# First token half's products issued ahead of the second half's transposes at the block ends

## The reference, cut to what matters

```python
def layer_norm(x, g, b):
    xf = x.astype(jnp.float32)
    mu = jnp.mean(xf, axis=-1, keepdims=True)
    var = jnp.mean(jnp.square(xf - mu), axis=-1, keepdims=True)
    return ((xf - mu) * lax.rsqrt(var + LN_EPS) * g + b).astype(x.dtype)

for i in range(DEPTH_2):                                      # DEPTH_2 = 2
    x = layer_norm(ALPHA * x + 0.5 * swiglu(x, ...), ...)     # ffn1
    proj = x @ rwkv_w_in[j]                                   # i = 0;  x @ sb_w_in[j] for i = 1
    ...
    x = layer_norm(ALPHA * x + heads @ w_out[i], ...)
    x = layer_norm(ALPHA * x + 0.5 * swiglu(x, ...), ...)     # ffn2
```

## Time and profile before

| | us |
|---|---|
| median of 3 runs | 1456.42 (1456.1 to 1458.33) |
| profiled execution, its own time | 1456.55 |
| its span in the trace | 1454.8 |
| PE busy | 1414.5 (97% of the span) |
| PEld busy | 1290.6 (89%) |
| DVE busy | 952.5 (65%) |
| ACT busy | 683.7 (47%) |
| granted TensorE clock, mean | 0.998 of full |

### The profile page before, as it was taken

How to read it: one execution, slowest core, us unless ns; L and a number is a source line. 1 busy time by engine, 2 the same in 40 slices (tenths; PEclk the granted TensorE clock), 3 DMA queues, 4 the chain that set the end, 5 groups by cost and what they waited for, 6 DMA issues and landing times.

```text
span 1454.8 us, 31311 instructions
## 1 busy us (share of the span) xinstructions
PE 1414.5 (97%) x12733; PEld 1290.6 (89%) x12733; DVE 952.5 (65%) x1290; ACT 683.7 (47%) x880; POOL 156.9 (11%) x182
## 2 busy tenths in 40 slices
PE   6999999999999999999989999999999999999997
PEld 5868799999999998988879999999999898899996
DVE  3657786667655556795786655675656778855656
ACT  5455654455433436743435433454334476534332
POOL 1442033221000004021300000000000011000000
PEclk9999999999999999999999999999999999999999
DMA  8975566666666645321036666566666344576662
GB/s 349 355 291 203 158 210 183 189 196 177 175 188 184 191 143 183 116 89 61 4 113 201 180 187 195 166 202 188 187 189 186 125 139 162 158 218 183 187 190 85
DMA packets 293910, 257.76 MB, mean 177 GB/s; under 512 B 7104, under 2 KB 270272, under 8 KB 290752
## 3 DMA queue, kind: packets, MB, share of 16 engines
q1 hardware_dynamic: 293824, 256.49, 57.5%
HBM read 255.42 MB, written 1.05 MB: 176 GB/s over the span
## 4 chain that ended last, share of the span: by engine, by line
PE 50%; DVE 4%; ACT 1%; issue 0%; DVEq 0%; ACTq 0%
PE ps L145 14%; PE ps L146 14%; PE ps L147 14%; PE ps L2331 3%; PE ps L383 1%; DVE stats L342 1%; DVE arena L340 1%; PE ps L390 1%; PE ps L469 0%; PE ps L474 0%; PE ps L470 0%; PE ps L2314 0%; PE ps L2322 0%; DVE gate_m L2634 0%; PE ps L2817 0%
## 5 line engine op out<-in xcount | busy, mean ns | idle before, releaser
L145 PE MATMUL ps<-actT,a_parts 128*128 128x256 f32 x2096 | 588.3, 281 | 2.9 <-DVE a_parts L130 2.0
L146 PE MATMUL ps<-actT,a_parts 128*128 128x256 f32 x2096 | 585.0, 279 | 0.0
L147 PE MATMUL ps<-actT,a_parts 128*128 128x256 f32 x2096 | 584.9, 279 | 0.0
L145 PEld LDWEIGHTS ps<-actT,a_parts 128*128 128x128 f32 x2096 | 394.0, 188 | 12.1 <-issue 3.8
L146 PEld LDWEIGHTS ps<-actT,a_parts 128*128 128x128 f32 x2096 | 393.8, 188 | 4.2
L147 PEld LDWEIGHTS ps<-actT,a_parts 128*128 128x128 f32 x2096 | 393.9, 188 | 0.0
L1350 DVE TENSOR_TENSOR a_parts<-a_raw,a_parts 128x2048 fp32r<-128x2048 f32 x100 | 238.4, 2384 | 54.5 <-ACT a_parts L1347 54.1
L1364 DVE TENSOR_TENSOR b_parts<-b_raw,b_parts 128x1024 fp32r<-128x1024 f32 x72 | 88.3, 1226 | 160.3 <-ACT b_parts L1361 160.3
L1347 ACT ACTIVATE a_parts<-a_raw 128x2048 fp32r<-128x2048 f32 x100 | 190.4, 1904 | 0.8 <-DMA a_raw<-in_ffn_w_up 0.8
L1361 ACT ACTIVATE b_parts<-b_raw 128x1024 fp32r<-128x1024 f32 x90 | 95.3, 1058 | 171.0 <-PE ps L147 171.0
L145 PE MATMUL ps<-b_parts,hid 128*128 128x512 f32 x400 | 158.1, 395 | 1.0 <-DVE hid L1461 1.0
(11 more groups left out here) (392 smaller groups left out, 1818.8 us busy)
## 6 DMA issues: line engine op xcount, KB each, us to landing
a_raw<-in_ffn_w_gate SPq DMA_DIRECT2D x88, 512.0 KB, 4.0
a_raw<-in_ffn_w_up SPq DMA_DIRECT2D x88, 512.0 KB, 5.2
b_raw<-in_ffn_w_down SPq DMA_DIRECT2D x88, 512.0 KB, 3.3
arena<-in_mod_w SPq DMA_DIRECT2D x24, 1024.0 KB, 10.1
a_raw<-in_f_up_w SPq DMA_DIRECT2D x44, 512.0 KB, 5.0
b_raw<-in_f_down_w SPq DMA_DIRECT2D x22, 512.0 KB, 3.3
a_raw<-in_rwkv_w_in SPq DMA_DIRECT2D x10, 1024.0 KB, 5.3
a_raw<-in_sb_w_in SPq DMA_DIRECT2D x10, 1024.0 KB, 5.1
```

The source lines that it names most:

```text
L145: pe.matmul(out, lhs[0], rhs[0], start=start, stop=False)
L146: pe.matmul(out, lhs[0], rhs[1], start=False, stop=False)
L147: return pe.matmul(out, lhs[1], rhs[0], start=False, stop=stop)
```

## The change

At all five hand-overs with a norm, the products of the first half's high part (`first_ahead`, 128 columns, both weight parts, eight k, so 16 per output) are issued before the second half's transposes, for the gate or the only output. In an FFN stage those of the up output follow the transposes, in the place of the four `keep_busy` products, which stay in the two projections. `first_products` then holds only the second half's 128 columns for the high part; the remainder's products stay 256 columns wide. Bank and columns of the results are the same. On DVE the remainder of the first half's six k moves ahead of all work on the second half.

```diff
@@ tokens_dve
             w = slice(t * P, (t + 1) * P)
+            dve.wait_ge(token_hi[0], i + 1)
+            first_lo(dve, yb, ACT_COLS).then_inc(token_lo[0], 1)
             dve.wait_ge(token_turned[t], 2 * i + 1)
...
                 dve.tensor_copy(actT[:, 0, pair, w], token_view(yb, t)[:, pair]).then_inc(pair_hi, 1)
-            dve.wait_ge(token_hi[0], i + 1)
-            first_lo(dve, yb, ACT_COLS).then_inc(token_lo[0], 1)
@@ first_products
                 if k == 0:
-                    pe.wait_ge(token_hi[0], i + 1)
-                    pe.wait_ge(token_lo[0], 2 * i + 2)
                     pe.wait_ge(pair_hi, 2 * i - 1)
...
                 for n, out_ in enumerate(outs):
                     w = weights(n, k)
-                    pe.matmul(out_, w[0], actT[:, 0, k], start=k == 0, stop=False)
-                    pe.matmul(out_, w[1], actT[:, 0, k], start=False, stop=False)
+                    for part in w:
+                        pe.matmul(out_[:, SECOND], part, actT[:, 0, k, SECOND], start=False, stop=False,
+                                  skip_group_check=True)
...
+        def first_ahead(pe, i, n, out_, weights):
+
+            for k in range(KD):
+                if k == 0:
+                    pe.wait_ge(token_hi[0], i + 1)
+                    pe.wait_ge(token_lo[0], 2 * i + 2)
+                for s, part in enumerate(weights(n, k)):
+                    pe.matmul(out_[:, FIRST], part, actT[:, 0, k, FIRST], start=k == 0 and s == 0, stop=False,
+                              skip_group_check=True)
@@ ffn_stage, TensorE
-                if take is not None:
+                if take is not None and got_norm is not None:
+                    pe.wait_ge(ring_a.lo_done, sa + 1)
+                    first_ahead(pe, got, 0, first_outs[0], first_weights)
                     turn_tokens(pe, got, 1)
-                    keep_busy(pe, 4 if got_norm is not None else 5)
+                    first_ahead(pe, got, 1, first_outs[1], first_weights)
@@ RWKV projection, TensorE (the stick-breaking one alike, with its own bank)
+                ring_a.wait_split(pe, g0)
+                first_ahead(pe, got, 0, chunk_bank(0)[:, 0], first_weights)
                 turn_tokens(pe, got, 1)
                 keep_busy(pe, 4)
```

More of the change, by code:

```diff
@@ L473, in first_products @@
                 for n, out_ in enumerate(outs):
-                    ins = pe.matmul(out_, weights(n, k)[0], actT[:, 1, k], start=False, stop=k == KD - 1)
-            return ins
+                    ins = pe.matmul(out_, weights(n, k)[0], actT[:, 1, k], start=False, stop=k == KD - 1,
+                                    skip_group_check=True)
+            return ins
+        def first_ahead(pe, i, n, out_, weights):
[5 more added lines that the diff above has]
+                    pe.matmul(out_[:, FIRST], part, actT[:, 0, k, FIRST], start=k == 0 and s == 0, stop=False,
+                              skip_group_check=True)
         def first_affine(eng, i, yb, norm, ks, scaled):
@@ L483, in first_affine @@
             return ins
-        FIRST = slice(0, P)
+        FIRST, SECOND = slice(0, P), slice(P, 2 * P)
         ACT_COLS, DVE_COLS = slice(0, 6), slice(6, KD)
@@ L517, in norm_dve_side @@
             block_low(dve, i, 1, yb)
-        SECOND = slice(P, 2 * P)
         QUADS = (slice(0, 4), slice(4, KD))
@@ L1470, in up_of, with first_weights @@
                 return ps[:, 1, SEQ:2 * SEQ] if kicked(q, j) else ps[:, 4 + q, SEQ:2 * SEQ]
+            first_outs = [ps[:, 4, 0:SEQ], up_of(0, 0)]
+            def first_weights(n, k):
+                return [a_parts[:, 0, s, n * BCH + k * P:n * BCH + (k + 1) * P] for s in range(2)]
             def up_first(pe):
-                gate, up = ps[:, 4, 0:SEQ], up_of(0, 0)
-                weights = lambda n, k: [a_parts[:, 0, s, n * BCH + k * P:n * BCH + (k + 1) * P] for s in range(2)]
                 if conv:
-                    ins = input_products(pe, gate, up, weights)
+                    ins = input_products(pe, *first_outs, first_weights)
                 else:
-                    pe.wait_ge(ring_a.lo_done, sa + 1)
-                    ins = first_products(pe, got, [gate, up], weights)
+                    ins = first_products(pe, got, first_outs, first_weights)
                 ins.then_inc(ring_a.used, 1)
@@ L1525, in _ @@
             def _(pe):
-                if take is not None:
+                if take is not None and got_norm is not None:
+                    pe.wait_ge(ring_a.lo_done, sa + 1)
+                    first_ahead(pe, got, 0, first_outs[0], first_weights)
                     turn_tokens(pe, got, 1)
-                    keep_busy(pe, 4 if got_norm is not None else 5)
+                    first_ahead(pe, got, 1, first_outs[1], first_weights)
+                elif take is not None:
+                    turn_tokens(pe, got, 1)
+                    keep_busy(pe, 5)
                 if kicked(0, 0):
@@ L1954, in project @@
                     if c == 0:
-                        first_products(pe, got, [chunk_bank(c)[:, 0]], lambda n, k: [
-                            ring_a.part(g0, s, k * P, k * P + P) for s in range(2)]).then_inc(ring_a.used, 1)
+                        first_products(pe, got, [chunk_bank(c)[:, 0]], first_weights).then_inc(ring_a.used, 1)
                         return
@@ L1969, in low_rank, with first_weights @@
                     ins.then_inc(norm_pe.up(name), 1)
+                def first_weights(n, k):
+                    return [ring_a.part(g0, s, k * P, k * P + P) for s in range(2)]
+                ring_a.wait_split(pe, g0)
+                first_ahead(pe, got, 0, chunk_bank(0)[:, 0], first_weights)
                 turn_tokens(pe, got, 1)
@@ L2784, in project @@
                     if c == 0 and n == 0:
-                        return first_products(pe, got, [ps[:, bank(c), 0:SEQ]], lambda n, k: [
-                            ring_a.part(g, s, k * 256, k * 256 + P) for s in range(2)])
+                        return first_products(pe, got, [ps[:, bank(c), 0:SEQ]], first_weights)
                     for k in range(KD):
@@ L2866, in behind, with first_weights @@
                         turn(4)
+                def first_weights(n, k):
+                    return [ring_a.part(g0, s, k * 256, k * 256 + P) for s in range(2)]
+                ring_a.wait_split(pe, g0)
+                first_ahead(pe, got, 0, ps[:, bank(0), 0:SEQ], first_weights)
                 turn_tokens(pe, got, 1)
```

## The result

The change made the kernel slower: 1467.34 us median of 6 runs (1465.86 to 1468.82) against 1458.34 of 6 runs before (1456.1 to 1458.78), ratio 1.0067, 95% interval 1.0056 to 1.0078, that is +9.8 us (8.2 to 11.4) by the ratio; the two medians lie 9.0 apart. The forecast was +9.4, from the 1456.42 us of the first three runs to 1465.8; the median of six runs before is 1.9 higher than that start, which is why the time lies 1.5 us over the forecast while the difference is met within 0.4.

What follows compares the result with a forecast made beforehand. TensorE's stream was taken as the bound on both sides of a hand-over. Three FFN hand-overs at +2.10 and two projections at +1.53 us gave +9.36, so 1465.8 us, own range 1464.2 to 1468.1, widened to 1460.0 to 1469.0.

Steps and rivals of the forecast that it cites:

- TensorE's stream is the bound behind the seam: At the hand-overs: what TensorE is late at the first whole-width product it stays late to the end.
- The rival of an absorbed delay at the projections: TensorE waits at the projections anyway, so only 6.3 us remain, 1462.7 us; chance 0.06.
- The price p of a narrow product: On TensorE, one product of 128 columns in a row costs 0.1075 us, ends 0.101 and 0.117, through its weight load.
- 240p - 16.44: The added time of all five hand-overs in us, with p the cost of one 128-column product; forecast +9.36.
- FFN hand-over, 64p + 2.78 = 9.66 us, +2.10: First moved product to steady work, at each of three FFN stages: 9.66 us against 7.56, +2.10, if no wait appears.
- Projection, 24p - 1.05 = +1.53: At each of two projections the last remainder product ends 1.53 us later, since the wait for the second half moves by 16p.
- DVE's move is worth nothing: At the FFN hand-overs, moving DVE's 0.95 us first-half remainder ahead gains nothing, as TensorE is not waiting for it.
- The sum: Three FFN hand-overs at 2.10 and two projections at 1.53 us: +9.36 us.
- The room of the second half's parts: At an FFN hand-over, 0.76 us or more of room would take most of a late start of L413.
- Only columns count: Rival: a narrow TensorE product costs p = 0.058 us, together -0.8 us, 1455.6 us; chance 0.12.
- The fall back to float32's way: Rival: each narrow TensorE product takes two instructions, p = 0.223 us, +37 us, 1493.5 us; chance 0.04.

Runs made afterwards that it cites:

- e5_widths: The changed kernel with the second half's high products at the three FFN hand-overs 64 token columns, 64 weight columns and 192 token columns; one run, 1468.51 us.
- e6_delay_only: The kernel before with eight more keep_busy products ahead of the second half's transposes at the five hand-overs; ratio 1.0058.
- e1: The changed kernel with DVE's remainder of the first half put back behind the second half's high parts, leaving only TensorE's half; ratio 1.0073.
- e4: The changed kernel with nine keep_busy products instead of fourteen in the ending stage; ratio 1.0046.
- e3: The changed kernel with the first half's products behind the second half's transposes, at the projections in place of the four keep_busy products; ratio 1.0051.
- e2: The kernel before with only DVE's half of the change, TensorE's stream as before; ratio 0.9998.

## Why the prediction was right, point by point

- *TensorE's stream is the bound behind the seam, so a delay stays.* Right: the delay alone gave +8.9 us for 5 x 1.78 put in, with no hand-over that kept back more than 0.03. The rival of an absorbed delay at the projections is shown wrong.
- *The price p of a narrow product.* The mechanism was right, the size a little low: 0.112 to 0.114 against 0.1075. I had taken the middle between L644's load (0.101) and the transposes (0.114), and the 0.101 was misread. It divides the row of eight L644 by eight, but a window that starts a little later leaves the first of them out and shows that the second starts 0.03 us behind it. Timeline of TensorE, kernel before, from 21.0 us:

```profile
20.77 0.92 PE L644 MATMUL ps<-arena 128*128 128x1 f32 x7
21.55 0.36 PE L145 MATMUL ps<-actT,a_parts 128*128 128x256 f32 x1
```

The other seven take 21.55 - 20.77 = 0.78 us, 0.111 each. So a single moving column costs the same as 64 to 192, and the nearest row of the kernel before had the right price in it: with 0.112 the forecast's own sum, 240p - 16.44, gives +10.4 us. The Trainium skill's figure for a weight load in TensorE: Matmul & The Clock Gate, section LDWEIGHTS, estimates 107 ns for 128 columns and 53 ns for 64; measured are distances of 0.112 and 0.061 us, 5 and 15% higher, the second of which may be that of the token columns. The fast weight load of the same page of the Trainium skill, section on weight-path perf modes, does not show: the distance is still 0.111 at 64 moving columns.
- *FFN hand-over, 64p + 2.78 = 9.66 us, +2.10.* Measured 9.96, +2.40, from the filler's end. The 64 narrow products took 1.82 + 1.81 + 3.58 = 7.21 us, 0.33 more than 64 x 0.1075; the transposes took 0.82 where 0.91 stood in the sum, the remainders 1.93 where 1.87 did. So the difference is p, but for 0.03. No wait appeared, as worked out; the parts of the second half were there each time. By the lengths of the table, from the filler's start, it is +2.33: what follows the filler starts 0.08 us sooner in the kernel after (3.04 us against 3.12), which I had not foreseen. The last filler product and the first L484 are 0.03 us apart, the last filler product and the first transpose of the kernel before 0.11.
- *Projection, 24p - 1.05 = +1.53.* Measured +1.60 at both from the filler's end (12.00 against 10.40 at the RWKV one), +1.51 and +1.52 from its start. With p at 0.112 it would be +1.64. I had taken ACT's L404, for k = 4, as what TensorE waits for; the wait that the timeline marks in the row of high products is for DVE's cast of k = 2, 3 (idle 0.17 us for L416 before, 0.24 for L418 after). Both parts come later by the same delay of the transposes, so the sum does not change by it.
- *DVE's move is worth nothing.* Said for the FFN hand-overs, and right there; at the projections, where I gave it no term, it is worth 0.2 us each.
- *The sum.* +9.4 forecast, +10.0 by the five lengths, +10.4 in the span, +9.8 by the ratio. The low p and the 0.08 us that each filler gives back work against each other: without the second, the five lengths would have come to +10.4.
- *The room of the second half's parts* was given as 0.76 us or more; the prediction's own times give 0.79 (771.26 - 770.47). Nothing hangs on it.
- *Only columns count* would have been about no change; the table of widths shows it wrong, with 0.111 at 64 columns. *The fall back to float32's way* did not happen: 16 products are 16 rows in the trace, 0.112 apart.

Where the gain that such a move promises went: the products were to use time in which TensorE had only filler, but each is half of a product whose other half costs as much as the whole. Of 32 wide products at 0.117 (3.81 us in the earlier trace rows) none got shorter, and 32 more came in.

## What to carry to other kernels

Before a product is split along its moving columns to start one part early, compare the weight load with the columns: for fp32r with 128 weight columns here everything up to 192 moving columns costs 0.112 us and 256 cost 0.117, so a half is nearly as dear as the whole, and even a first half that is wholly hidden saves 0.005 us per product. A quarter of the product, 64 weight columns by 128 moving ones, costs 0.061, which is half of the whole, so cutting it in both directions does not pay either; 64 weight columns by all 256 moving ones were not measured. When such a price is read from a merged row, look at the first distance apart from the others: in a row of eight it took 0.101 for 0.112. And look whether the moved work really replaces the filler or stands behind it; here that was worth 0.75 us per hand-over.

## What the runs showed of the hardware that was not expected

Where products of one kind follow those of another, a single distance can be 0.03 us instead of 0.11: it is so between the first two of L644, between the filler and L484 (the filler's 28 products take 3.04 us there and 3.12 ahead of the transposes) and between the transposes and L484 (0.82 us for the eight and 0.91 before). Why is open.

Once the clock fell while TensorE worked without a gap. In e5_widths the granted clock went to the lower of its two levels during the stretch of 64-column products. Windows view (busy us and counts of PE, PEld, DVE, ACT, POOL, then granted clock, DMA share, GB/s):

```profile
772.50:775.00 2.50, 2.50 (x26) 2.50 (x24) 1.39 (x5) 2.50 (x3) 0.00 (x0) 1.00 0.00 0
775.00:780.00 5.00, 5.00 (x26) 5.00 (x26) 4.56 (x4) 3.07 (x3) 0.00 (x0) 0.53 0.11 21
776.70:780.20 3.50, 3.50 (x17) 3.50 (x18) 2.86 (x3) 1.37 (x2) 0.00 (x0) 0.50 0.19 41
```

Ahead of the fall TensorE had issued 64-column products 0.111 us apart, busy all the time by its rows; after it the 256-column products of L474 ran 0.22 us apart (776.67 to 780.23 for 16) instead of 0.117, at 1.2 GHz. The hand-over took 15.27 us for it, against 13.00 in the kernel after. At the other four hand-overs of this profile, and at all five of the kernel after, the clock was full, with 128 or 192 columns at the same distance. But this is one stretch of one run, and the clock fell elsewhere too, without such products (next); that the 64 columns brought it down is not shown.

The profiled span of some variants exceeds what their hand-overs account for, and shorter falls of the clock stand in the same profiles. In e6_delay_only (span 1466.8, 12.0 over before, for 8.9 put in):

```profile
596.00:604.00 8.00, 8.00 (x59) 8.00 (x58) 6.44 (x8) 6.62 (x9) 0.00 (x0) 0.79 0.43 133
732.00:744.00 12.00, 10.19 (x224) 9.45 (x221) 7.07 (x13) 2.44 (x5) 0.00 (x0) 0.86 0.58 178
```

The kernel before shows 1.00 in both stretches of its profile, and so does the kernel after. They lie in the RWKV stage, far from any edit; e1 and e4 show the same two (0.79 and 0.86), e3 the first alone. From chunk 2 of the RWKV projection to the next long filler, a stretch that holds both places, it takes

| | falls | us |
|---|---|---|
| before, after, e2, e5 | none | 196.98, 197.77, 197.31, 196.72 |
| e3 | one | 198.49 |
| e1, e4, e6 | two | 199.63, 198.54, 199.63 |

so the profiles with a fall are 0.7 to 2.9 us longer there than those without; another part of e4's excess lies at its start, where the first long filler stands at 553.77 us against 552.42 before. By the mean clocks the falls are no fixed part of a variant: the five runs of e1 have spans of 1465.0 and 1465.8 us at a mean granted clock of 0.999 and of 1467.3 to 1468.1 at 0.996 to 0.997, and the profiled run was the longest of the five in e1, e4 and e6. So a variant is to be judged by its ratio or by its hand-overs, and not by the span of one profile. What starts such a fall is open.
